# Seven products for eight in 27 groups of the down-projections of a two-block kernel, the sums into the residual shared between VectorE and GpSimd

## The chip, the cores and the metric

The kernel runs on one core of one Trainium2 chip. The metric is the time of one execution on the device in microseconds (us), lower is better; where several executions are given, the median counts. TensorE does the matmuls (PE in the profile, its weight loads PEld), VectorE is DVE, ScalarE is ACT, GpSimd is POOL, and SyncE (SP) issues most of the DMAs.

## The reference, cut to what matters

One sequence of 256 tokens of width 2048 in fp32 goes through two blocks. The first is stick-breaking attention and an MLP with a squared relu, the second is chunked attention beside a pooling branch, and an MLP with a causal convolution of width 3 and a gate:

```python
# first block (D_FF = 8192)
h = h + stick_breaking_mixer(rms_norm(h, norm_mix), sb_w_qkv, sb_w_o)
h = h + jnp.square(jax.nn.relu(rms_norm(h, norm_mlp) @ mlp_w1)) @ mlp_w2
x = rms_norm(h, final_norm)
# second block (D_FF_2 = 5632)
x = x + rms_norm_2(jnp.concatenate([a, p], axis=-1) @ w_o, post_mix_g)
up = causal_dwconv(rms_norm_2(x, pre_ffn_g) @ w_up, conv_w, conv_b)
y = (jax.nn.gelu(up[..., :D_FF_2], approximate=True) * up[..., D_FF_2:]) @ w_down
x = x + rms_norm_2(y, post_ffn_g)
```

The change is in the two down-projections, `mlp_w2` (8192 x 2048) and `w_down` (5632 x 2048), and in what makes their inputs.

## The kernel before

**Tiling.** All weights are streamed from HBM once. The unit is a *piece*: 256 rows of a weight matrix by 512 columns (a *strip* is 512 columns, with 8 pieces for a matrix of 2048 rows). Each weight and each activation is used as two fp32r parts, high and low: ScalarE copies the raw piece, rounded, into `Wh` (L986), and VectorE subtracts to get `Wl` (L1204); together this is the *split* of a piece. A plain piece has 12 matmuls of 128x512: for each row of 128 tokens and each 128 weight rows, high x high, high x low and low x high (`row_products`, through the helper at L1546). The two rows of tokens add up in the two banks of `ps0` or `ps1`; the four banks of `ps2` serve side work.

**Order.** `plan_program` writes the order of all engines by hand: a list of pieces, and steps of each engine that are put `after` a given piece or `later` by some pieces. The plan splits piece i+4 just ahead of the products of piece i. `Wh` and `Wl` have 5 buffers, so a split of piece i waits until piece i-5 has been multiplied, and the raw pieces have 6 buffers, with the load of the next piece into a buffer issued by SyncE once the `Wl` of the last one is there. Every engine works its own steps in order. A step that waits holds up all behind it on its engine.

**Up-projections.** In the first MLP 16 strips of `mlp_w1` are done in chunks of 6, 5 and 5, in the second 11 pairs of strips of `w_up` in chunks of 6 and 5. The output of a strip makes a *trip*: ScalarE stages it in `T0` (L1042 or L1044), two DMAs pass it to DRAM, four DMAs bring it back in another shape (the step `land_rows`, L917), and VectorE transposes it into `T1` (L1256, `turn_strip`). One trip is under way at a time; a trip is landed 3 pieces after its start and turned 4 pieces later. In the first MLP the squared relu is taken on the way and `hid_halves` (L1084, L1325) splits the result into `hid1`. In the second MLP a trip is followed by the convolution, four instructions of ScalarE (L1125) and eight of VectorE (L1416) with one split in between; the first strip of a pair ends in `gelu` (L1129), the second in `gate`, a product of GpSimd (L1529), and `gate_halves` (L1133, L1422) splits its result into `hid2`, two pieces after the gate.

**Down-projections.** After each chunk, four strips of the down-projection use the 12 (or 10) pieces that belong to the chunk, in two pairs of strips (`strip_pair`), and `add_products`, `y_first` or `y_sum` adds the two banks of a strip into the residual `xN` (first MLP, L1283) or into `xn`, which lies in `QK` (second MLP, L1427, L1440). In the second chunk of the second MLP `y_sum` is followed by a product of GpSimd (L1534).

## Time and profile before

| | |
|---|---|
| median of 3 runs | 2095.36 us (2094.35 to 2097.16) |
| the profiled execution | 2095.49 us |
| its span in the profile | 2093.8 us |
| PE busy | 2083.5 us |
| DVE busy | 1224.2 us |
| ACT busy | 1072.2 us |
| POOL busy | 119.7 us |
| read from HBM | 432.75 MB |

The span is the time from the first to the last instruction in the trace; the profiled execution took 1.7 us more than that. A row of a timeline gives start and duration of one instruction, or of several of one form that are merged into a row (x3), and in brackets how long the engine had been idle before it and what ended that wait. Instructions of VectorE that follow each other overlap a little: three splits of 1.23 us stand as 3.49 us. Where the text speaks of the place of piece n after a known time, each plain piece is 12 matmuls.

### The profile page before, as it was taken

Reading aid. Unit: us, or ns where it says so; the run is one execution under the profiler, and the core shown is the slowest. Engines: PE = TensorE matmul, PEld = TensorE weight load, DVE = VectorE, ACT = ScalarE, POOL = GpSimd, SP = SyncE. Lnnn points to the kernel's source line nnn. Section 1 sums busy time; section 2 is a strip of 40 time slices with the busy share of each in tenths; the row PEclk is TensorE's granted clock in tenths of the full one; section 3 lists DMA queues with packets and bytes.
Section 4 is the critical chain, followed back from the end, with each engine's and each line's share of the span. In section 5 each row is a group of like instructions: output and inputs, shape, how many; then the busy total and the mean of one; then the engine's idle time right before and its main releaser. Section 6 shows DMA issues by size and latency. Waiting matters only on the chain.

```text
span 2093.8 us, 23749 instructions
## 1 busy us (share of the span) xinstructions
PE 2083.5 (100%) x9304; PEld 1728.1 (83%) x9304; DVE 1224.2 (58%) x1312; ACT 1072.2 (51%) x1303; POOL 119.7 (6%) x66
## 2 busy tenths in 40 slices
PE   9999999999999999999999999999999999999998
PEld 8888888888888888888888888888888888888887
DVE  6546556655554555455566755566666654566665
ACT  7555654555434543455455554455555533555553
POOL 3000000000000000000002000000112100011120
PEclk9999999999999999999999999999999999999999
DMA  8688666888667885688588777667878766787863
GB/s 297 197 251 236 191 188 216 260 248 235 211 193 206 241 254 194 196 243 238 192 270 232 229 244 232 197 203 211 249 236 250 220 211 193 223 247 242 251 221 121
DMA packets 291903, 469.46 MB, mean 224 GB/s; under 512 B 18512, under 2 KB 82128, under 8 KB 291280
## 3 DMA queue, kind: packets, MB, share of 16 engines
q1 hardware_dynamic: 290928, 463.46, 72.5%
q10 hardware_dynamic: 864, 4.49, 0.6%
q8 instruction: 73, 1.20, 0.2%
q14 instruction: 38, 0.31, 0.0%
HBM read 432.75 MB, written 35.13 MB: 223 GB/s over the span
## 4 chain that ended last, share of the span: by engine, by line
PE 96%; DVE 1%; DMA 1%; ACT 1%; issue 0%; SPq 0%; ACTq 0%; DVEq 0%
PE ps L1546 96%; DMA T<-passed_strip 1%; DVE Wl L1204 0%; DVE zs L1416 0%; ACT Wh L986 0%; DMA E<-passed_rows 0%; DVE T L1256 0%; DMA gains<-in_gains_dram 0%; DVE E L1416 0%; ACT zs L1125 0%; SPq L917 0%; DMA passed_rows<-xN 0%; ACT T L1044 0%; DVE aHL L1307 0%; PE ps L1549 0%
## 5 line engine op out<-in xcount | busy, mean ns | idle before, releaser
L1204 DVE TENSOR_TENSOR Wl<-raw,Wh 128x1024 fp32r<-128x1024 f32 x743 | 908.2, 1242 | 674.2 <-ACT Wh L986 673.6
L1546 PE MATMUL ps<-Wh,aHL 128*128 128x512 f32 x3712 | 1148.8, 390 | 2.4 <-DVE Wl L1204 0.8
L986 ACT ACTIVATE Wh<-raw 128x1024 fp32r<-128x1024 f32 x743 | 768.0, 1054 | 611.1 <-PE ps L1546 608.7
L1546 PEld LDWEIGHTS ps<-Wh,aHL 128*128 128x128 f32 x3712 | 696.8, 188 | 147.9 <-DVE Wl L1204 1.3
L1546 PE MATMUL ps<-Wl,aHL 128*128 128x512 f32 x1856 | 722.1, 389 | 0.0
L1546 PE MATMUL ps<-Wh,hid 128*128 128x512 f32 x1728 | 532.8, 389 | 0.0
L1546 PEld LDWEIGHTS ps<-Wl,aHL 128*128 128x128 f32 x1856 | 348.4, 188 | 71.8
L1546 PEld LDWEIGHTS ps<-Wh,hid 128*128 128x128 f32 x1728 | 324.3, 188 | 67.4
L1546 PE MATMUL ps<-Wl,hid 128*128 128x512 f32 x864 | 336.1, 389 | 0.0
L1546 PEld LDWEIGHTS ps<-Wl,hid 128*128 128x128 f32 x864 | 162.2, 188 | 33.7
L1546 PE MATMUL ps<-Wh,oHL 128*128 128x512 f32 x512 | 159.0, 390 | 0.0
L1546 PEld LDWEIGHTS ps<-Wh,oHL 128*128 128x128 f32 x512 | 96.1, 188 | 20.0
L1529 POOL TENSOR_TENSOR E<-E,zs 128x1024 f32<-128x1024 f32 x11 | 60.9, 5534 | 794.8 <-DVE E L1416 794.8
L1546 PE MATMUL ps<-Wl,oHL 128*128 128x512 f32 x256 | 99.6, 389 | 0.0
L1256 DVE STREAM_TRANSPOSE T<-T 128x1024 f32<-128x1024 f32 x38 | 47.2, 1242 | 17.1 <-DMA T<-passed_strip 17.1
L1546 PEld LDWEIGHTS ps<-Wl,oHL 128*128 128x128 f32 x256 | 48.1, 188 | 9.8
L1044 ACT ACTIVATE T<-ps,rs 128x512 f32<-128x512 f32 x72 | 46.0, 676 | 15.6 <-PE ps L1546 7.9
L1520 POOL TENSOR_TENSOR QK<-E 128x1020 f32<-128x1020 f32 x2 | 3.8, 1886 | 821.6 <-DVE E L1256 821.6
L1125 ACT ACTIVATE E<-T,conv 128x256 f32<-128x256 f32 x44 | 22.9, 590 | 44.5 <-DVE T L1256 44.5
L1133 ACT ACTIVATE hid<-E 128x1024 fp32r<-128x1024 f32 x11 | 11.7, 1061 | 65.6 <-POOL E L1529 65.6
L1125 ACT ACTIVATE zs<-T,conv 128x256 f32<-128x256 f32 x44 | 22.9, 590 | 31.9 <-DVE T L1256 31.9
L1084 ACT ACTIVATE hid<-T 128x1024 fp32r<-128x1024 f32 x16 | 17.0, 1062 | 39.2 <-DVE T L1256 39.2
(167 smaller groups left out, 687.4 us busy)
## 6 DMA issues: line engine op xcount, KB each, us to landing
raw<-in_mlp_w_dram SPq DMA_DIRECT2D x256, 512.0 KB, 4.5
raw<-in_w_up_dram SPq DMA_DIRECT2D x176, 512.0 KB, 4.6
raw<-in_sb_w_qkv_dram SPq DMA_DIRECT2D x93, 512.0 KB, 5.2
raw<-in_w_down_dram SPq DMA_DIRECT2D x88, 512.0 KB, 4.7
raw<-in_w_in_dram SPq DMA_DIRECT2D x64, 512.0 KB, 4.8
passed_strip<-T SPq DMA_DIRECT2D x104, 256.0 KB, 4.5
T<-passed_strip SPq DMA_DIRECT2D x208, 128.0 KB, 5.2
raw<-in_sb_w_o_dram SPq DMA_DIRECT2D x32, 512.0 KB, 5.4
```

Of the source, the lines that this page charges most:

```text
L986: e.activation(Wh[:, i % NW, :], rawv[:, i % NRAW, :], ACT.Copy).then_inc(st["hi"][0], 1)
L1044: e.activation(strip_rows[:, t, :], ps[st["set"]][:, t, :], ACT.Copy, scale=cols[st["col"]][:, t:t + 1]).then_inc(st["staged"][t][0], 1)
L1084: e.activation(hid1[:, st["t0"]:st["t0"] + 4, 0:TOK], T1[:, :, :], ACT.Copy).then_inc(st["hi"][0], 1)
L1125: e.activation(C[:, m, :], T1[:, m, :], ACT.Identity, scale=conv[:, 2, n0 + m:n0 + m + 1], bias=conv[:, 3, n0 + m:n0 + m + 1]).then_inc(st ...
L1133: e.activation(hid2[:, st["t0"]:st["t0"] + 4, 0:TOK], E4, ACT.Copy).then_inc(st["hi"][0], 1)
L1204: e.tensor_tensor(Wl[:, i % NW, :], rawv[:, i % NRAW, :], Wh[:, i % NW, :].bitcast(F32), ALU.subtract).then_inc(st["lo"][0], 1)
L1256: e.transpose(dst, strip_blocks).then_inc(st["done"][0], 1)
L1520: e.tensor_tensor(dst[:, a:4, sh:TOK], src[:, a:4, sh:TOK], src[:, a:4, 0:TOK - sh], ALU.add).then_inc(added[0], 1)
L1529: e.tensor_tensor(E4, E4, Z4, ALU.mult).then_inc(st["done"][0], 1)
L1546: return e.matmul(o, l, r, start=start, stop=stop, skip_group_check=True)
```

## The change

A *group* takes one pair of pieces, the same 256 weight rows of two neighbouring strips (a, b), and computes their eight half products (two rows of tokens, two halves of the 256 weight rows, two strips) as seven products of sums, in the manner of Strassen and Winograd. It is four entries in the list of pieces: `s0`, `s1`, `s2` with 6 matmuls each and `s3` with 3, together 21 where two plain pieces have 24. There are 27 groups: three in each pair of strips of every chunk of both down-projections, but for the last pair of `mlp_w2`. Groups are spaced by 3 or 2 plain pieces.

Around a group the change adds:

- `weight_sums`: four additions of 128x512 on VectorE, from the two raw pieces into the new tile `wsum` (the second writes into the raw piece), ahead of the split of `s0`; `s1` to `s3` are split from these sums (`s2` 1024 wide, `s3` 512 wide).
- `mix_tokens` and `mix_low`: the sums of the activations, four instructions of VectorE, one of ScalarE and one more of VectorE, once for groups 0 and 1 of a chunk (`n=2`) and once for group 2 (`n=1`); they stand behind `hid_halves` and `gate_halves` of the first two results of a chunk. `gate_halves` itself moves back by a piece in all rounds.
- `fold`: the four banks of `ps2`, in which the groups of a pair of strips add up, are brought into the residual: one copy by ScalarE, and eight additions. In the 7 folds that add to a residual, VectorE makes five and GpSimd three (`fold_rest`); in the two of the first chunk of `w_down`, which begin `xn`, VectorE makes all. `add_products`, `y_first` and `y_sum` wait for the fold, and the next `weight_sums` or `mix_tokens` wait for it too.
- the row factor of the first MLP is applied in the relu, and no longer as its square in `add_products`.

The core of the diff:

```diff
@@ strip_pair, seven @@
+    def strip_pair(w, s4, ks, tail, mov, tiles, evacs, koff=0, sevens=(), fold=None):
+        plain = [kp for kp in ks if kp not in sevens]
...
+        lead, gap = (4, 3) if tail else (2, 3 if len(plain) > 7 else 2)
+        rest = a[lead:n] + b[:n] if tail else a[lead:n - 1] + b[:2] + a[n - 1:] + b[2:]
+        p.pieces[first:] = a[:lead]
+        for m, kp in enumerate(sevens):
+            seven(w, s4, kp, mov, tiles, (a[0]["strip"], b[0]["strip"]), koff, m, m == 0, fold if m == len(sevens) - 1 else None)
+            p.pieces += rest[gap * m:gap * m + gap] if m < len(sevens) - 1 else rest[gap * m:]
+        p.pieces += a[n:] + b[n:] if tail else []
...
+        for i, kind in enumerate(("s0", "s1", "s2", "s3")):
+            src = (w, "rows", kp * 256, (s4 + i) * STRIP) if i < 2 else None
@@ evac_relu and gated @@
+                if t0 < 8:
+                    free["T1"] = [lo, mix_tokens("hid1", "T1", t0 // 2, 2 if t0 == 0 else 1, [turned])]
...
+                    if t0 < 8:
+                        free["E"] = [lo, mix_tokens("hid2", "E", t0 // 2, 2 if t0 == 0 else 1, [g])]
                     hid_tiles[t0:t0 + 4] = [lo] * 4
-                later(2, halves)
+                later(3, halves)
@@ the pairs of mlp_w2 and w_down @@
+                           sevens=() if c == 2 and s4 else tuple(range(2 * at, 2 * at + 3)), fold=fold_into("xN", s4))
...
+                           sevens=tuple(range(2 * at, 2 * at + 3)), fold=fold_into("xn", s4, fresh=c == 0))
@@ vector_program @@
+                elif k == "weight_sums":
...
+                    e.tensor_tensor(wsum[:, 0, :], a[:, 0, :], b[:, 0, :], ALU.add).then_inc(made[1][0], 1)
+                    e.tensor_tensor(b[:, 0, :], b[:, 0, :], b[:, 1, :], ALU.add).then_inc(made[3][0], 1)
+                    e.wait_ge(*made[1])
+                    e.tensor_tensor(wsum[:, 1, :], wsum[:, 0, :], b[:, 1, :], ALU.add).then_inc(made[2][0], 1)
+                    e.wait_ge(*made[2])
+                    e.tensor_tensor(wsum[:, 2, :], wsum[:, 1, :], a[:, 1, :], ALU.add).then_inc(made[4][0], 1)
+                elif k == "mix_tokens":
...
+                    e.tensor_tensor(d[:, :, 1, :], even[:, :, 0:128], even[:, :, 128:256], ALU.subtract).then_inc(st["d"][0][0], 1)
+                    e.tensor_tensor(d[:, :, 0, :], even[:, :, 128:256], odd[:, :, 128:256], ALU.subtract).then_inc(st["d"][1][0], 1)
...
+                    e.wait_ge(*st["d"][2])
+                    e.tensor_tensor(d[:, :, 3, :], d[:, :, 2, :], odd[:, :, 0:128], ALU.add).then_inc(st["d"][3][0], 1)
+                elif k == "mix_low":
...
+                    e.tensor_tensor(lo, d, hi.bitcast(F32), ALU.subtract).then_inc(st["lo"][0], 1)
+                elif k in ("fold", "fold_rest"):
...
+                        e.tensor_tensor(wsum[:, 0, :], P[:, 0, :], wsum[:, 0, :], ALU.add).then_inc(m[0][0], 1)
...
+                            e.tensor_tensor(x[:, 0, a], x[:, 0, a], P[:, 0, :], ALU.add).then_inc(m[1][0], 1)
+                            e.wait_ge(*m[0])
+                            e.tensor_tensor(wsum[:, 1, :], P[:, 2, :], wsum[:, 0, :], ALU.add).then_inc(m[2][0], 1)
+                            e.tensor_tensor(wsum[:, 2, :], P[:, 1, :], wsum[:, 0, :], ALU.subtract).then_inc(m[3][0], 1)
...
+                        e.tensor_tensor(wsum[:, 0, :], P[:, 1, :], wsum[:, 1, :], ALU.subtract).then_inc(m[4][0], 1)
@@ scalar_program @@
+                elif k == "fold":
...
+                    e.activation(wsum[:, 0, :], ps[2][:, 3, :], ACT.Copy).then_inc(st["copied"][0], 1)
+                elif k == "mix_tokens":
+                    d, hi, lo = mixed_rows(st)
+                    e.wait_ge(*st["d"][3])
+                    e.activation(hi, d, ACT.Copy).then_inc(st["hi"][0], 1)
@@ pool_program @@
+                elif k == "fold_rest" and not st["fresh"]:
...
+                    e.wait_ge(*m[2])
+                    e.tensor_tensor(x[:, 1, a], x[:, 1, a], wsum[:, 1, :], ALU.add).then_inc(added[0][0], 1)
+                    e.wait_ge(*m[3])
+                    e.tensor_tensor(x[:, 0, b], x[:, 0, b], wsum[:, 2, :], ALU.add).then_inc(added[1][0], 1)
+                    e.wait_ge(*m[4])
+                    e.tensor_tensor(x[:, 1, b], x[:, 1, b], wsum[:, 0, :], ALU.add).then_inc(added[2][0], 1)
@@ tensor_program @@
+                terms = {"s0": (("a11", side[:, 0, :], q["opens"], True), ("a12", a[:, 0, :], False, False)),
+                         "s1": (("d1", side[:, 2, :], q["opens"], True), ("d3", b[:, 0, :], q["opens"], False)),
+                         "s2": (("d0", side[:, 1, :], q["opens"], True), ("d2", side[:, 3, :], q["opens"], True)),
+                         "s3": (("a22", a[:, 1, :], False, False),)}[q["kind"]]
+                for t, (name, P, starts, ends) in enumerate(terms):
+                    c = slice(t * 512, (t + 1) * 512)
+                    x, h, l = halves_of[name]
+                    mm(P, x[:, h:h + 128], wh[:, c], starts, False)
+                    mm(P, x[:, h:h + 128], wl[:, c], False, False)
+                    m = mm(P, x[:, l:l + 128], wh[:, c], False, ends and q["closes"])
```

**How the steps stand on VectorE, first place.** These are VectorE's instructions in the first round of `w_up`, before. The convolutions into `E` and then into `zs` belong to the second strip of the first pair and the first strip of the second; `hid<-E` is `gate_halves`, and `Wl<-raw,Wh` are splits.

```order
L1416 SCALAR_TENSOR_TENSOR E<-T,conv,E 128x254 x2
L1204 TENSOR_TENSOR Wl<-raw,Wh 128x1024 x3
L1422 TENSOR_TENSOR hid<-E,hid 128x4x256
L1204 TENSOR_TENSOR Wl<-raw,Wh 128x1024 x3
L1256 STREAM_TRANSPOSE T<-T 128x1024
L1204 TENSOR_TENSOR Wl<-raw,Wh 128x1024
L1416 SCALAR_TENSOR_TENSOR zs<-T,conv,zs 128x255 x2
```

The same place in the changed kernel:

```order
L1578 SCALAR_TENSOR_TENSOR E<-T,conv,E 128x254 x2
L1323 TENSOR_TENSOR Wl<-raw,Wh 128x1024 x4
L1584 TENSOR_TENSOR hid<-E,hid 128x4x256
L1341 TENSOR_TENSOR wsum<-E 128x2x128
L1342 TENSOR_TENSOR wsum<-E 128x2x128
L1344 SCALAR_TENSOR_TENSOR wsum<-wsum,E 128x2x128
L1347 TENSOR_TENSOR wsum<-wsum,E 128x2x128
L1323 TENSOR_TENSOR Wl<-raw,Wh 128x1024
L1351 TENSOR_TENSOR hidMix<-wsum,hidMix 128x8x128
L1323 TENSOR_TENSOR Wl<-raw,Wh 128x1024
L1422 STREAM_TRANSPOSE T<-T 128x1024
L1323 TENSOR_TENSOR Wl<-raw,Wh 128x1024
```

One split has moved ahead of `gate_halves`, and the five instructions of the mix stand between it and the transpose. On ScalarE, whose order at that place is the second piece, the high part of the mix stands ahead of the next two splits:

```order
L1251 ACTIVATE hid<-E 128x4x256
L1103 ACTIVATE hidMix<-wsum 128x8x128
L1099 ACTIVATE Wh<-raw 128x1024 x2
L1243 ACTIVATE zs<-T,conv 128x256 x4
L1099 ACTIVATE Wh<-raw 128x1024
```

Before, three splits stood there between the first row and the four of the convolution, and no mix.

**Second place.** VectorE where the first `w_down` begins, before: the last trip of the chunk (transpose, split, convolution), its gate's halves, and then splits up to `y_first`.

```order
L1256 STREAM_TRANSPOSE T<-T 128x1024
L1204 TENSOR_TENSOR Wl<-raw,Wh 128x1024
L1416 SCALAR_TENSOR_TENSOR E<-T,conv,E 128x255 x2
L1416 SCALAR_TENSOR_TENSOR E<-T,conv,E 128x254 x2
L1416 SCALAR_TENSOR_TENSOR E<-T,conv,E 128x255 x2
L1416 SCALAR_TENSOR_TENSOR E<-T,conv,E 128x254 x2
L1204 TENSOR_TENSOR Wl<-raw,Wh 128x1024 x3
L1422 TENSOR_TENSOR hid<-E,hid 128x4x256
L1204 TENSOR_TENSOR Wl<-raw,Wh 128x1024 x11
```

The same place in the changed kernel, from the four sums of the second group on:

```order
L1422 STREAM_TRANSPOSE T<-T 128x1024
L1329 TENSOR_TENSOR wsum<-raw 128x512
L1330 TENSOR_TENSOR raw<-raw 128x512
L1332 TENSOR_TENSOR wsum<-wsum,raw 128x512
L1334 TENSOR_TENSOR wsum<-wsum,raw 128x512
L1323 TENSOR_TENSOR Wl<-raw,Wh 128x1024
L1578 SCALAR_TENSOR_TENSOR E<-T,conv,E 128x255 x2
L1578 SCALAR_TENSOR_TENSOR E<-T,conv,E 128x254 x2
L1578 SCALAR_TENSOR_TENSOR E<-T,conv,E 128x255 x2
L1578 SCALAR_TENSOR_TENSOR E<-T,conv,E 128x254 x2
L1323 TENSOR_TENSOR Wl<-raw,Wh 128x1024
L1323 TENSOR_TENSOR Wl<-wsum,Wh 128x1024
```

The last transpose now falls just ahead of the second group's sums, and the whole convolution stands between the splits of that group's `s0` and `s1`. `hid<-E` follows behind the splits of `s1`, `s2`, `s3` and one plain piece.

## Rows read from the trace of the kernel before

**Rows 1.** The page, part 1: busy time of each engine, share, instructions.

```profile
PE 2083.5 (100%) x9304; PEld 1728.1 (83%) x9304; DVE 1224.2 (58%) x1312; ACT 1072.2 (51%) x1303; POOL 119.7 (6%) x66
```

**Rows 2.** Waits of PE: who was waited for, us in total, times, longest.

```profile
PE ps L1546 <- DVE Wl L1204: 0.8, 1, 0.8
```

**Rows 3.** The chain that ended last, in order of time: start, us, what.

```profile
1464.97 620.47 PE ps L1546 x2736
```

**Rows 4.** Groups of VectorE and ScalarE by form: busy us, mean ns, idle before.

```profile
L1204 DVE TENSOR_TENSOR Wl<-raw,Wh 128x1024 fp32r<-128x1024 f32 x743 | 908.2, 1242 | 674.2 <-ACT Wh L986 673.6
...
L1286 DVE TENSOR_TENSOR xN<-xN,ps 128x512 f32<-128x512 f32 x8 | 5.1, 681 | 0.0
```

**Rows 5.** Timeline of VectorE in the first round of w_up.

```profile
1443.35 3.49 DVE L1204 TENSOR_TENSOR Wl<-raw,Wh 128x1024 fp32r<-128x1024 f32 x3
1450.22 1.23 DVE L1422 TENSOR_TENSOR hid<-E,hid 128x1024 fp32r<-128x1024 f32 x1 [3.38 <-ACT hid L1133]
...
1455.05 1.25 DVE L1256 STREAM_TRANSPOSE T<-T 128x1024 f32<-128x1024 f32 x1 [0.20 <-DMA T<-passed_strip]
...
1460.54 3.24 DVE L1416 SCALAR_TENSOR_TENSOR zs<-T,conv,zs 128x255 f32<-128x255 f32 x8
1463.69 1.22 DVE L1204 TENSOR_TENSOR Wl<-raw,Wh 128x1024 fp32r<-128x1024 f32 x1
```

**Rows 6.** Timeline of ScalarE at the same place.

```profile
1449.12 1.06 ACT L1133 ACTIVATE hid<-E 128x1024 fp32r<-128x1024 f32 x1 [7.26 <-POOL E L1529]
```

**Rows 7.** Timeline of PE at the end of that stretch.

```profile
1464.97 0.50 PE L1546 MATMUL ps<-Wh,aHL 128*128 128x512 f32 x1 [0.84 <-DVE Wl L1204]
```

**Rows 8.** Timeline of VectorE: the split behind the convolution, in three later rounds.

```profile
1505.70 1.22 DVE L1204 TENSOR_TENSOR Wl<-raw,Wh 128x1024 fp32r<-128x1024 f32 x1
...
1852.31 1.22 DVE L1204 TENSOR_TENSOR Wl<-raw,Wh 128x1024 fp32r<-128x1024 f32 x1
...
1895.22 1.23 DVE L1204 TENSOR_TENSOR Wl<-raw,Wh 128x1024 fp32r<-128x1024 f32 x1
```

**Rows 9.** Timeline of GpSimd: first and last gate of the first chunk.

```profile
1444.00 5.09 POOL L1529 TENSOR_TENSOR E<-E,zs 128x1024 f32<-128x1024 f32 x1 [288.90 <-DVE E L1416]
...
1658.87 5.58 POOL L1529 TENSOR_TENSOR E<-E,zs 128x1024 f32<-128x1024 f32 x1 [39.02 <-DVE E L1416]
```

**Rows 10.** Timeline of GpSimd: an addition of 128x1020.

```profile
1122.86 1.89 POOL L1520 TENSOR_TENSOR QK<-E 128x1020 f32<-128x1020 f32 x1 [805.04 <-DVE E L1256]
```

**Rows 11.** Timeline of VectorE: a split that begins inside that GpSimd instruction.

```profile
1123.12 2.71 DVE L1204 TENSOR_TENSOR Wl<-raw,Wh 128x1024 fp32r<-128x1024 f32 x1 [0.34 <-ACT Wh L986]
```

**Rows 12.** Timeline of VectorE from the last trip of the first chunk of w_up.

```profile
1650.06 1.25 DVE L1256 STREAM_TRANSPOSE T<-T 128x1024 f32<-128x1024 f32 x1 [2.86 <-DMA T<-passed_strip]
1654.41 1.22 DVE L1204 TENSOR_TENSOR Wl<-raw,Wh 128x1024 fp32r<-128x1024 f32 x1 [3.10 <-ACT Wh L986]
1655.55 3.24 DVE L1416 SCALAR_TENSOR_TENSOR E<-T,conv,E 128x255 f32<-128x255 f32 x8
1658.70 3.49 DVE L1204 TENSOR_TENSOR Wl<-raw,Wh 128x1024 fp32r<-128x1024 f32 x3
```

**Rows 13.** Timeline of SyncE: landing DMAs of the last trip of each chunk.

```profile
1640.26 1.97 SPq L917 DMA_DIRECT2D T<-passed_strip  x4
...
1987.35 2.57 SPq L917 DMA_DIRECT2D T<-passed_strip  x4
```

**Rows 14.** Timeline of VectorE: the transpose behind the second of them.

```profile
1996.42 1.25 DVE L1256 STREAM_TRANSPOSE T<-T 128x1024 f32<-128x1024 f32 x1 [1.06 <-DMA T<-passed_strip]
```

**Rows 15.** The page, part 6: DMAs of one line, KB each, median us to landing.

```profile
T<-passed_strip SPq DMA_DIRECT2D x208, 128.0 KB, 5.2
```

**Rows 16.** GpSimd: products and sums of 128x512, by form.

```profile
L1534 POOL TENSOR_TENSOR QK<-QK,g_row 128x512 f32<-128x512 f32 x6 | 7.7, 1298 | 43.4 <-ACT T L1139 43.4
L1494 POOL TENSOR_TENSOR E<-E 128x512 f32<-128x512 f32 x2 | 3.7, 1828 | 24.2 <-ACT E L990 24.2
```

**Rows 17.** Timeline of VectorE: a transpose in the first MLP.

```profile
467.81 1.24 DVE L1256 STREAM_TRANSPOSE T<-T 128x1024 f32<-128x1024 f32 x1
```

227 lines of the change are left out of this document (173 added, 54 removed).

## The prediction

> **What bounds the kernel now.** The page's busy times come first: PE is busy for 2083.5 us of a span of 2093.8, DVE for 1224.2 [rows 1]. Next the waits of PE: in the middle of the program there is one of note, 0.8 us on the low half of a weight piece [rows 2]. So the kernel is bound by the number of matmuls. Their price is in the chain of waits: 2736 of them in a row take 620.47 us [rows 3], 0.2268 us each, and a plain piece of 12 takes 2.721 us with no loss between pieces. That row also gives a clock for the text: piece n after 1464.97 starts at 1464.97 + 2.721 n. The last thing to read is who is nearly late. VectorE splits a piece in 1.15 us when splits follow each other (three in 3.49 [rows 5]; 1.24 alone [rows 4]), under half of what PE takes for it, but its queue is in order, and in each round of `w_up` it waits for a DMA, for ScalarE and for GpSimd in turn. The reader should look there for the slack, not at the share of 58%.
>
> **What is removed.** A group has 21 matmuls for 24: 27 x 3 = 81 matmuls x 0.2268 = **18.4 us less** on PE. PE has no other work to put there, so the whole of it is on the path as long as each split is there in time. Loads from HBM are unchanged. The weights of a group reach VectorE and ScalarE as two raw pieces as before.
>
> **What is added where it is hidden.** Four sums of 128x512 cost 0.68 each alone, as the nearest additions do [rows 4], some 2.5 together. `s2` and `s3` add a split of 1.15 and one of half the size, 0.6. That is 4.2 us more on VectorE for each group. Between groups: with three plain pieces PE takes 4.76 + 8.16 = 12.9 us and VectorE 10.0, with two 10.2 and 8.9. Both fit, so a row of groups by itself takes no time. In the order of the buffers the tightest split (the first plain one behind `s3`, which waits for the piece five before it) is ready some 2.4 us early. The first groups of the first MLP meet a transpose and its halves, VectorE's queue being some 7.3 us long from the transpose to the split of `s0`. The transpose needs no wait at 467.81, 18.6 us behind its strip's end [rows 17]; here it can start at 15.8, so the split ends at 23.1, and PE wants it at 23.8: nothing lost, 0 to 1 us for all three chunks. The sums of the activations in the first MLP are hidden too, since there the splits run a full four pieces ahead. The relu of the first MLP now takes the row factor as a scale, on ScalarE, which has room there: no cost on the path.
>
> **The fold.** ScalarE's copy and VectorE's five additions read PSUM. GpSimd's three are 1.30 each at the best and 1.83 on average in the worst row [rows 16]. Here the two engines shut each other out: a split that begins 0.26 us into a GpSimd addition takes 2.71 instead of 1.23, and ends 1.1 after that addition [rows 10, 11]. And GpSimd gets nothing done while splits of VectorE follow each other: the gate at 1658.87 takes 5.58 us, of which three splits fill the first 3.3 (to 1662.19), and it ends 2.26 after them [rows 9, 12]. So three additions on GpSimd (3.9) take more of what the engines share than on VectorE (1.8 to 2.0). The Trainium skill (*GPSIMD Engine Reference*, section 4.1, Engine selection) speaks against this move: element-wise work with two inputs belongs on VectorE, GpSimd being about twice as slow. By that factor and the 0.68 of rows 4 an estimate is 4.1 us for the three against the 3.9 of rows 16, and the sum below would stay. Who waits: `add_products`, with VectorE's whole queue behind it. Before the last two groups' pairs that matter (second chunk of each MLP, where only two plain pieces lie between the fold and `add_products`) I reach: additions done 9.8 us after the fold's start, the sums at 13.6, `s0` split at 14.8 against 16.3, `s2` at 18.3 against 19.1. Slack 0.8: **0 us**, bounds 0 and 4 (two places x 2).
>
> **The first mix in `w_up` (n=2).** Here nothing is hidden, since PE already waits 0.84 [rows 7] for the split behind the convolution [rows 5]. `gate_halves` stands one split later. ScalarE's part of it begins when GpSimd is done, at 1449.12 [rows 6]; the gate takes from 1444.00 to there [rows 9], 2.26 behind the third split. Now a fourth split follows without a gap, its high part being long ready, so the gate ends 1.15 later. Then, on VectorE: low half of the gate to 1452.5; the four sums at 0.4 to 0.5 (the eight of the convolution take 3.24 [rows 5]) to 1454.3; ScalarE's high part of the mix 1.06 and the high part of the next split 1.0, both exposed, to 1456.3; split to 1457.6, low part of the mix to 1458.7, split to 1459.9. The transpose starts 4.8 us later than at 1455.05, and all behind it too. PE loses **4.8** (3.6 if the gate is not held).
>
> The second mix (n=1) has half the width or less: 3.5 late by the same steps. The split behind its convolution ends at 1506.92 and PE wants it at 1508.51 [rows 8]: slack 1.6, loss **1.9** (0.8 to 1.9). In the second chunk the split ends at 1853.53, with PE at 1464.97 + 144 x 2.721 = 1856.85: slack 3.3 [rows 8], loss **1.5** (0 to 1.7). The fourth would have 3.9 [rows 8], but after a round with no slack the trips are late, and the first chunk shows that a round wins back 1.6: loss between 0 and 1.9, I take **1.0**. Together 9.2.
>
> **The last trip against the second group of `w_down`.** Before, the first `w_down` starts at 1464.97 + 60 x 2.721 = 1628.25. Its last trip is transposed at +21.8, and the split behind the convolution ends 9.8 after that, at +31.6, with PE there at +32.7 [rows 12]. Slack 1.0. In the change PE comes to the same place in VectorE's queue (`s1` of the second group) after 7 plain pieces, 21 matmuls and the 6 of `s0`, at +25.2, or 7.5 us sooner. The trip lands earlier as well, since fewer pieces stand ahead of it on SyncE: by the steps above the split of the first group's `s1` ends at +12.0, and the landing DMAs go then (before: at +12.0 in the first chunk, +10.8 in the second [rows 13]; there I find 10.7). From first issue to the transpose it is 9.8 and 9.1 [rows 12 to 14], at least 2.0 + 5.2 = 7.2 [rows 13, 15]. With two loads just ahead instead of three I take 8: the transpose L is at +20.1 and +18.7. The four sums hide behind ScalarE's half of the convolution, so `s1` is there at L + 9.9: 4.8 and 3.4 late. Then the gate: four splits follow each other (4.1 us), GpSimd needs 2.25 behind them, ScalarE 1.1 for the halves and 1.0 for the next split, VectorE's low halves the rest, which makes L + 18.6 for a piece that PE would want at +31.3. The second wait comes on top: in all L - 12.7, or **7.4** and **6.0**, 13.4 us (bounds: L from 17.2 in both, 9.0; L of 21.9 and 19.7, 16.2).
>
> **The sum.** Against the profiled execution, 2095.5 (span 2093.8, and 1.7 around it, 0.1 above the median of 2095.36): 2095.5 - 18.4 + 9.2 + 13.4 = 2099.7, and with 0.3 for the first MLP **2100**. The gain is real and PE hands all of it back waiting for VectorE.
>
> **The rivals.**
> 1. *The lead holds.* If trips land at L = 17.2, the gates are not held back by a fourth split and the three later mixes stay in their slack, the losses are 3.6 + 0.8 + 0.4 + 9.0 = 13.8, which gives 2091; with no wait at all it is 2077. For it: PE's waits before were a single 0.84, and I count every wait from durations of one trace. Against it: the 7.5 us by which PE arrives sooner are sure. Chance 0.22, 2077 to 2091.
> 2. *GpSimd's three additions become the bound.* In the two places with two plain pieces ahead of `add_products`, a slower addition moves `s2` past PE, from a lateness of 0.8 us on. At 1.83 each [rows 16] the three end 1.6 later and a place loses 0.8; at 2.7, as long as the split that was shut out [rows 11], it loses 3.4. Two such places and landings at 9.8 give 2104 to 2110. Chance 0.13. It ends slower.
> 3. *Entries of 3 and 6 matmuls do not run at the pitch of 12.* Rows 3 show no loss at a boundary, which speaks against it; at 0.1 us for each of 54 more boundaries 2105. Chance 0.05.
> 4. The forecast, 2093 to 2106, chance 0.60.
>
> **How the numbers follow.** A measurement of this kernel can tell about 0.2%, 4.2 us: from 2091.2 to 2099.6 is no change. The forecast lies just above that bound; of its 0.60 I give 0.28 to the same and 0.32 to slower. Rival 1 is faster, rivals 2 and 3 slower: faster 0.22, same 0.28, slower 0.50. The range takes in most of rival 1's upper end and rival 2: 2088 to 2108.
>
> **What would show it.** PE's matmuls fall by 81, its busy time by some 18 if waits are not counted as busy. PE's waits should name the low half of the weights four times in `w_up` (4.8 first) and twice in each `w_down`, behind the convolution (3 to 5) and behind `gate_halves` (2 to 3). The first gate should take 6.2 instead of 5.1 us, and transposes behind a mix come 3.5 to 5 later against PE. The forecast is wrong if the second group's `s1` is there before PE, if ScalarE's mix does not hold its next split, or if `add_products` waits for GpSimd until PE runs dry.

## The result and the profile after

The changed kernel takes **2123.9 us** (median of 4 runs, 2122.3 to 2126.9) where the kernel before, timed beside it, takes 2096.3: a ratio of 1.0133, with a 95% interval of 1.0115 to 1.0150. It is 28 us slower. The forecast was 2100, in a range of 2088 to 2108: the sign was the likelier one, the size was not.

The page of the changed kernel, part 1, against [rows 1]: 81 matmuls fewer, VectorE 169 us busier, GpSimd 52 us busier. The span is 2120.5.

```profile
PE 2082.5 (98%) x9223; PEld 1717.3 (81%) x9223; DVE 1393.3 (66%) x1568; ACT 1129.4 (53%) x1376; POOL 171.6 (8%) x87
```

PE's busy time hardly fell (2083.5 to 2082.5), though 81 matmuls at 0.2268 should take 18.4 off it. That is the first sign of something besides the waits shown. PE's waits, against the single one of [rows 2]:

```profile
PE ps L1722 <- DVE Wl L1323: 26.2, 19, 4.7
PE ps L1722 <- DVE QK L1606: 2.9, 2, 2.4
```

The row of 620 us without a break [rows 3] is gone. In the chain of waits of the changed kernel other engines stand between shorter rows of matmuls (start, us, what):

```profile
1645.39 9.27 DMA T<-passed_strip
1660.25 3.17 DVE E L1578 x8
1663.48 6.17 POOL E L1705
1673.19 159.43 PE ps L1722 x702
```

**Where it went.** The trace gives the number of matmuls up to any time. The time lost in a stretch is how much later the last of its matmuls comes, with 0.2268 us credited for each one that the change saved before it (readings from windows 2.5 us apart, good to some 0.3 us, and to 0.8 where a wait falls between two stretches; what the kernel before itself lost counts as zero, so its own wait of 0.84 can show as a gain). The same for the experiments that are told below:

| us lost in | change | fold on VectorE | mixes alone | groups in first MLP only | w_down: second pair only | w_down: first pair only | third chunk plain | causes removed |
|---|---|---|---|---|---|---|---|---|
| first MLP, chunks 1 and 2 | 1.1 | 0.0 | 0.0 | 1.6 | 2.0 | 1.6 | 1.1 | 1.1 |
| third chunk, pair 1 | 1.8 | 0.7 | 0.2 | 0.0 | 0.3 | 0.5 | 0.0 | 0.0 |
| third chunk, pair 2 | 4.1 | 3.7 | -0.2 | -0.2 | 4.3 | 3.9 | -0.2 | -0.2 |
| w_up, chunk 1 | 7.1 | 6.2 | 8.0 | -1.1 | 6.8 | 6.6 | 6.2 | 7.1 |
| w_down, chunk 1, pair 1 | 10.7 | 9.1 | 0.2 | 1.6 | 0.1 | 10.7 | 9.1 | 1.6 |
| w_up, chunk 2 | 1.7 | 3.1 | 4.4 | 0.1 | 2.8 | 3.1 | 5.6 | 1.9 |
| w_down, chunk 2, pair 1 | 11.6 | 12.0 | 1.6 | 0.2 | 1.8 | 15.5 | 13.2 | 0.0 |
| w_down, chunk 2, pair 2 | 7.6 | 5.7 | 0.1 | 0.3 | 2.6 | -0.2 | 8.1 | 1.9 |

What is left of each column (attention, the second pair of the first chunk of w_down) is a gain of 0.5 to 1.0 in all. In the change everything comes to 44.8; less 18.4 it is 26.4 of the 26.7 us between the two spans.

The 1.8 in the first pair of the third chunk is a wait of PE of 1.26 at 989.46, 18 us before that pair's fold. The last trip of the chunk landed late there: VectorE waited 1.63 for the DMA before its transpose at 982.04, with the sums and the split of a group behind it. Five other kernels run the same program up to there (experiments 4, 6, 7, 9 and 13), and in their traces PE has no wait over 0.2 at that place. So it belongs to this one execution, and not to the fold.

**The first mix** in w_up, against [rows 5] to [rows 7]. Timelines of GpSimd, VectorE and PE in the changed kernel (start, us, engine, line, what, and in brackets the idle time before it and what ended that):

```profile
1439.31 6.56 POOL L1705 TENSOR_TENSOR E<-E,zs 128x1024 f32<-128x1024 f32 x1 [287.36 <-DVE E L1578]
1447.00 1.23 DVE L1584 TENSOR_TENSOR hid<-E,hid 128x1024 fp32r<-128x1024 f32 x1 [3.38 <-ACT hid L1251]
1451.77 1.23 DVE L1323 TENSOR_TENSOR Wl<-raw,Wh 128x1024 fp32r<-128x1024 f32 x1 [2.08 <-ACT Wh L1099]
1455.18 1.24 DVE L1422 STREAM_TRANSPOSE T<-T 128x1024 f32<-128x1024 f32 x1
1453.05 0.50 PE L1722 MATMUL ps<-Wh,aHL 128*128 128x512 f32 x1 [0.85 <-DVE Wl L1323]
1460.80 0.80 PE L1722 MATMUL ps<-Wh,aHL 128*128 128x512 f32 x1 [2.00 <-DVE Wl L1323]
```

The gate begins 4.7 us sooner than before and takes 6.56 instead of 5.09; the transpose stands at 1455.18 and not at 1455.05, so it has lost 4.8 us to the gate, as forecast. PE waits 2.85 in all there, and the stretch loses 4.1: the clock, told below, takes another 1.7.

**The start of the first w_down**, against [rows 12] and [rows 13]. PE comes to 1631.4 there. Timelines of SyncE (the landing DMAs of the last trip), VectorE, then PE:

```profile
1643.90 1.95 SPq L1024 DMA_DIRECT2D T<-passed_strip  x4
1654.69 1.25 DVE L1422 STREAM_TRANSPOSE T<-T 128x1024 f32<-128x1024 f32 x1 [6.10 <-DMA T<-passed_strip]
1659.03 1.23 DVE L1323 TENSOR_TENSOR Wl<-raw,Wh 128x1024 fp32r<-128x1024 f32 x1 [0.59 <-ACT Wh L1099]
1663.32 1.22 DVE L1323 TENSOR_TENSOR Wl<-raw,Wh 128x1024 fp32r<-128x1024 f32 x1
1660.40 0.76 PE L1722 MATMUL ps<-Wh,hid 128*128 128x512 f32 x1 [4.74 <-DVE Wl L1323]
1664.60 0.80 PE L1722 MATMUL ps<-Wh,hidMix 128*128 128x512 f32 x1 [1.30 <-DVE Wl L1323]
```

The two splits are those of the second group's `s0`, with the four sums ahead of it, and of its `s1`, with the convolution ahead of it. The first matmul behind each wait takes 0.76 and 0.80 where 0.50 is usual. The windows around it tell why (from:to, length, busy time and count of PE, PEld, DVE, ACT and POOL, granted clock of TensorE, DMA share, GB/s):

```profile
1650.00:1658.00 8.00, 5.66 (x25) 4.34 (x24) 3.28 (x5) 2.03 (x5) 0.00 (x0) 1.00 0.72 209
1658.50:1669.00 10.50, 7.30 (x16) 5.30 (x17) 8.39 (x13) 3.86 (x5) 5.51 (x1) 0.51 0.34 107
1669.00:1680.00 11.00, 10.90 (x48) 8.67 (x47) 9.19 (x10) 7.42 (x8) 0.65 (x1) 1.00 0.48 157
```

The granted clock falls from 1.00 to 0.50, that is from 2.4 to 1.2 GHz, in the middle of the wait and stays there until 1669: 16 matmuls in 7.3 us where full speed makes twice as many. That is 3.6 us lost on top of the waits. In windows of half a microsecond the same shows in three other places: 1460.8 to 1464.2, 2017.2 to 2024.0 and 2102.5 to 2105.9. The kernel before has it only at its very end. Half of the matmul time in them is 1.7, 2.5 and 1.7: together with the 3.6 some **9.5 us**, a fifth of the 44.8 lost, and one half of why PE's busy time did not fall. No term of the forecast had it.

**The fold of the third chunk**, where the next pair has no group. Timelines of GpSimd, VectorE, PE:

```profile
1011.03 1.29 POOL L1697 TENSOR_TENSOR xN<-xN,wsum 128x512 f32<-128x512 f32 x1 [167.81 <-DVE wsum L1366]
1012.29 2.27 POOL L1699 TENSOR_TENSOR xN<-xN,wsum 128x512 f32<-128x512 f32 x1
1014.52 2.27 POOL L1701 TENSOR_TENSOR xN<-xN,wsum 128x512 f32<-128x512 f32 x1
1013.93 1.71 DVE L1323 TENSOR_TENSOR Wl<-raw,Wh 128x1024 fp32r<-128x1024 f32 x1
1016.99 1.29 DVE L1448 TENSOR_TENSOR xN<-xN,ps 128x512 f32<-128x512 f32 x2 [1.35 <-PE ps L1722]
1020.10 1.23 DVE L1323 TENSOR_TENSOR Wl<-raw,Wh 128x1024 fp32r<-128x1024 f32 x1 [1.82 <-ACT Wh L1099]
1024.34 1.23 DVE L1323 TENSOR_TENSOR Wl<-raw,Wh 128x1024 fp32r<-128x1024 f32 x1 [1.81 <-ACT Wh L1099]
1028.58 1.23 DVE L1323 TENSOR_TENSOR Wl<-raw,Wh 128x1024 fp32r<-128x1024 f32 x1 [1.82 <-ACT Wh L1099]
1029.86 0.50 PE L1722 MATMUL ps<-Wh,hid 128*128 128x512 f32 x1 [0.36 <-DVE Wl L1323]
```

`add_products` (L1448) is put down as waiting for PE, but the strip's last matmul ended at about 1012.7; what ended at 1016.79 is GpSimd's third addition. From there on VectorE splits a piece only every 4.24 us, since each split stands behind an addition and, on ScalarE, behind the squares of its result; PE takes one every 2.72 and catches up at 1029.86. The kernel before runs the same chain, but its `add_products` begins at 1019.97, as soon as the strip is done, and so the chain has four to five more microseconds in hand. GpSimd's first addition takes 1.29, its second and third 2.27, in this fold as in all seven.

**The last pair of w_down**: the same chain with `y_sum`, in two places. At the front of the pair it is `y_sum` of the pair before, behind that pair's fold, with this pair's first group in it. The first wait of PE is for `y_sum` itself: a group writes the sums of both strips, and so needs early the banks that `y_sum` still reads. Timelines of VectorE, ScalarE, PE:

```profile
2050.38 1.29 DVE L1606 TENSOR_TENSOR QK<-QK,ps 128x512 f32<-128x512 f32 x2 [1.28 <-POOL QK L1701]
2058.60 1.28 DVE L1606 TENSOR_TENSOR QK<-QK,ps 128x512 f32<-128x512 f32 x2
2059.31 0.63 ACT L1257 ACTIVATE T<-QK 128x512 f32<-128x512 f32 x1 [4.24 <-DVE QK L1606]
2061.84 2.52 DVE L1323 TENSOR_TENSOR Wl<-wsum,Wh 128x1024 fp32r<-128x1024 f32 x2 [1.96 <-ACT Wh L1099]
2059.93 0.50 PE L1722 MATMUL ps<-Wh,hid 128*128 128x512 f32 x1 [2.44 <-DVE QK L1606]
2063.81 0.50 PE L1722 MATMUL ps<-Wh,hidMix 128*128 128x512 f32 x1 [0.85 <-DVE Wl L1323]
```

Near its end it is the pair's own fold, whose last addition on GpSimd ends at 2095.92, and the `y_sum` behind it. Timelines of VectorE and PE:

```profile
2096.92 1.27 DVE L1606 TENSOR_TENSOR QK<-QK,ps 128x512 f32<-128x512 f32 x2
2100.16 1.88 DVE L1323 TENSOR_TENSOR Wl<-raw,Wh 128x1024 fp32r<-128x1024 f32 x1 [1.96 <-ACT Wh L1099]
2102.09 0.50 PE L1722 MATMUL ps<-Wh,hid 128*128 128x512 f32 x1 [1.95 <-DVE Wl L1323]
```

This wait, with the 1.7 of half clock behind it, is 3.8 of the 7.6 us, one half.

### The profile page after: what moved, and what is told of

Its sections match the earlier page's. It is cut to its first block, busy times and chain, and to the rows that moved or that the text cites. A ratio compares the mean times of both kernels' runs of the same rounds, so it can differ in the third digit from the quotient of the medians.

```text
span 2120.5 us, 24084 instructions
## 1 busy us (share of the span) xinstructions
PE 2082.5 (98%) x9223; PEld 1717.3 (81%) x9223; DVE 1393.3 (66%) x1568; ACT 1129.4 (53%) x1376; POOL 171.6 (8%) x87
## 4 chain that ended last, share of the span: by engine, by line
PE 75%; DVE 10%; DMA 5%; ACT 4%; issue 2%; POOL 2%; SPq 1%; ACTq 0%; DVEq 0%; POOLq 0%
PE ps L1722 75%; DVE Wl L1323 4%; DMA T<-passed_strip 4%; ACT Wh L1099 2%; POOL E L1705 2%; DVE E L1578 1%; DVE zs L1578 1%; DVE T L1422 1%; SPq L1024 1%; ACT zs L1243 1%; ACT E L1243 0%; ACT hid L1251 0%; DMA passed_rows<-xN 0%; SPq L1045 0%; DVE wsum L1332 0%
## 5 line engine op out<-in xcount | busy, mean ns | idle before, releaser
L1722 PE MATMUL ps<-Wh,hid 128*128 128x512 f32 x1458 | 461.5, 392 | 19.4 <-DVE Wl L1323 16.1
L1722 PEld LDWEIGHTS ps<-Wh,hid 128*128 128x128 f32 x1458 | 275.1, 189 | 83.8 <-issue 12.9
L1722 PE MATMUL ps<-Wl,hid 128*128 128x512 f32 x729 | 285.1, 391 | 0.0
L1722 PEld LDWEIGHTS ps<-Wl,hid 128*128 128x128 f32 x729 | 137.7, 189 | 28.1
L1705 POOL TENSOR_TENSOR E<-E,zs 128x1024 f32<-128x1024 f32 x11 | 71.5, 6499 | 802.3 <-DVE E L1578 802.3
L1722 PE MATMUL ps<-Wh,hidMix 128*128 128x512 f32 x216 | 74.2, 405 | 4.1 <-DVE Wl L1323 4.1
L1099 ACT ACTIVATE Wh<-wsum 128x1024 fp32r<-128x1024 f32 (+1 forms) x54 | 44.1, 838 | 26.5 <-PE ps L1722 26.0
L1722 PEld LDWEIGHTS ps<-Wh,hidMix 128*128 128x128 f32 x216 | 42.3, 196 | 15.0 <-DVE Wl L1323 5.9
L1323 DVE TENSOR_TENSOR Wl<-wsum,Wh 128x1024 fp32r<-128x1024 f32 (+1 forms) x54 | 50.3, 966 | 6.3 <-ACT Wh L1099 6.3
```

The source lines that it names most:

```text
L1099: e.activation(Wh[:, i % NW, c], src, ACT.Copy).then_inc(st["hi"][0], 1)
L1323: e.tensor_tensor(Wl[:, i % NW, c], src, Wh[:, i % NW, c].bitcast(F32), ALU.subtract).then_inc(st["lo"][0], 1)
L1705: e.tensor_tensor(E4, E4, Z4, ALU.mult).then_inc(st["done"][0], 1)
L1722: return e.matmul(o, l, r, start=start, stop=stop, skip_group_check=True)
```

## The experiments

All are built from the changed kernel unless the text says otherwise, and each was timed beside the kernel before.

**1. All additions of a fold on VectorE.** This undoes what gives the change its name, and no more.

```diff
@@ vector_program, fold_rest @@
                         e.tensor_tensor(wsum[:, 0, :], P[:, 1, :], wsum[:, 1, :], ALU.subtract).then_inc(m[4][0], 1)
+                        e.tensor_tensor(x[:, 1, a], x[:, 1, a], wsum[:, 1, :], ALU.add).then_inc(added[0][0], 1)
+                        e.tensor_tensor(x[:, 0, b], x[:, 0, b], wsum[:, 2, :], ALU.add).then_inc(added[1][0], 1)
+                        e.wait_ge(*m[4])
+                        e.tensor_tensor(x[:, 1, b], x[:, 1, b], wsum[:, 0, :], ALU.add).then_inc(added[2][0], 1)
```

> The changed kernel with all eight additions of a fold on VectorE. Theory 1 (GpSimd's additions and VectorE shut each other out, and that is a third of what was lost): the fold's additions end earlier in the second chunk of w_down, its second pair of strips loses 2 to 4 us and not 7.6, the last pair of the first MLP's third chunk 2 and not 4.1, and the time is 2114 to 2119. Theory 2 (what is late is VectorE's whole queue, and three more additions of 0.7 us there cost what GpSimd's cost): 2122 to 2127. The losses in the rounds of w_up (4.1 and 3.0) and at the start of the first w_down (10.7) stay in both, since no fold with GpSimd stands there.

Measured: 2118.05, ratio 1.0109 (1.0095 to 1.0122) against 1.0133: **5 to 6 us back**, theory 1 in the total. By the table at most 3.4 of it lie where additions of GpSimd are waited for (1.1 in the first two chunks, 0.4 in the third chunk's second pair, 1.9 in the last); the rest moved too: 2.5 less in w_up and w_down of the first chunk, where GpSimd adds nothing, 1.1 less in the wait at 989.46, and 1.8 more in the second chunk up to the end of its first pair. The fold of the third chunk in this kernel, timeline of VectorE, where the additions take 0.69 each and `add_products` (now L1453) follows without a wait, 2.9 us sooner than in the change:

```profile
1011.72 0.69 DVE L1377 TENSOR_TENSOR xN<-xN,wsum 128x512 f32<-128x512 f32 x1
1012.32 0.69 DVE L1379 TENSOR_TENSOR xN<-xN,wsum 128x512 f32<-128x512 f32 x1
1012.92 1.22 DVE L1323 TENSOR_TENSOR Wl<-raw,Wh 128x1024 fp32r<-128x1024 f32 x1
1014.05 1.28 DVE L1453 TENSOR_TENSOR xN<-xN,ps 128x512 f32<-128x512 f32 x2
```

But the two pairs still lose 3.7 and 5.7, not 2 and 2 to 4. PE too is 2.3 us sooner here, so little of that lead is kept, and the chain of splits at 4.24 us is late whoever adds. GpSimd is at most a fifth of the loss, not a third.

**2. The mixes alone.** No group at all; the sums of the activations are made and not used, and `gate_halves` stays a piece later. (`sevens=()` in both down-projections.)

> The changed kernel with every group replaced by its two plain pieces, the sums of the activations kept (made and not used), gate_halves still a piece later. Theory 1 (the sums of the activations are late by themselves): w_up loses 4.1 + 3.0 + 1.7 = 8.8 us as it does with groups, and where w_down begins there is no wait over 1 us, which gives 2096.3 + 8.8 - 0.8 = 2104. Theory 2 (they only cost together with groups, since it is the groups of the first MLP that use up the lead): 2096 to 2098, with no wait over 1.5 us in w_up.

Measured: 2108.8, ratio 1.0066 (1.0053 to 1.0080): **13.6 us** over the kernel before, more than either theory gave. No group is needed for the loss in w_up. It is 8.0 in the first chunk, and in the second 4.4 where the change itself lost 1.7, with 1.6 more where w_down begins. Two of PE's waits in this kernel:

```profile
1463.77 0.50 PE L1725 MATMUL ps<-Wh,aHL 128*128 128x512 f32 x1 [1.98 <-DVE Wl L1323]
1468.07 0.50 PE L1725 MATMUL ps<-Wh,aHL 128*128 128x512 f32 x1 [1.25 <-DVE Wl L1323]
```

**3. Groups in the first two chunks of the first MLP only**: 12 of 27, and no mixes in w_up.

```diff
-                           sevens=() if c == 2 and s4 else tuple(range(2 * at, 2 * at + 3)), fold=fold_into("xN", s4))
+                           sevens=() if c == 2 else tuple(range(2 * at, 2 * at + 3)), fold=fold_into("xN", s4))
...
-                           sevens=tuple(range(2 * at, 2 * at + 3)), fold=fold_into("xn", s4, fresh=c == 0))
+                           sevens=(), fold=fold_into("xn", s4, fresh=c == 0))
...
-                    if t0 < 8:
+                    if t0 < 0:
                         free["E"] = [lo, mix_tokens("hid2", "E", t0 // 2, 2 if t0 == 0 else 1, [g])]
...
-                later(3, halves)
+                later(2, halves)
```

> Groups in the first and second chunk of the first MLP's down-projection alone (12 of the 27), no group and no sums of activations elsewhere, gate_halves where it was before. Theory 1 (a group that meets slack gives its 0.68 us back whole, and these 12 do): 36 matmuls less, 2096.3 - 8.2 = 2088, with no new wait of PE. Theory 2 (part of what was lost later was brought on by these groups, by loads and trips that come out of step): 2091 to 2096, with waits in the third chunk at 989 and 1030 to 1052.

Measured: **2087.5** (2087.1 to 2089.2), ratio 0.9963 (0.9949 to 0.9976). Theory 1. It beats both kernels, the one before by 7.7 us where its 36 matmuls are worth 8.2. VectorE's weights hold PE up for

```profile
PE ps L1725 <- DVE Wl L1323: 1.2, 1, 1.2
```

and the clock shows no fall.

**4. Groups in w_down's second pairs only**: the six groups of the first pairs plain (`sevens=() if s4 == 0 else ...`).

> The changed kernel with the six groups of the first pair of strips plain in both chunks of w_down, the rest as it was. Theory 1 (the 10.7 and 11.6 us lost where a w_down begins come from the groups that meet the last trip and its gate there): 6 x 0.68 = 4.1 us more matmuls, 20 to 22 us less waiting, 2104 to 2108, and no granted clock at its lower level where w_down begins. Theory 2 (they come from the trips and gate_halves being late already behind w_up's sums of activations): 2122 to 2128, the wait of 4.7 us still there. The 7.6 us of the second chunk's second pair stay in both.

Measured: 2102.8, ratio 1.0034 (1.0021 to 1.0048). Theory 1, and a little more: 4.1 us of matmuls come back in and the time still falls by 21, so **25 us** of loss go with the six groups. The starts of w_down lose 0.1 and 1.8, the granted clock stays at 1.00 there, and the last pair loses 2.6, not 7.6, though its own groups stay. That part of the expectation missed: the 7.6 did not stay. What is left is the wait behind the pair's own fold, again 1.95 long (at 2082.65), this time with no fall of the clock.

**5. `gate_halves` a piece later, in the kernel before, and nothing else** (`later(2, halves)` to `later(3, halves)`).

> The kernel before with one edit: gate_halves a piece later, in all rounds. The sums of the activations with this edit, without groups, cost 13.6 us. Theory 1 (the sums themselves cost that; the later gate_halves only holds the first gate by one more split, 1.15 us, where PE already waited 0.84): 2096 to 2098. Theory 2 (gate_halves moved past a split is late in every round and takes a good part of the 13.6): 2100 to 2104, with waits of PE in most rounds of w_up.

Measured: 2096.2 against 2095.8, ratio 1.0002 (0.9993 to 1.0011). Theory 1: no cost. The 13.6 of experiment 2 are the mixes' own.

**6. `gate_halves` back in its place, in the changed kernel** (`later(3, halves)` to `later(2, halves)`).

> The changed kernel with gate_halves where it was before (two pieces after the gate, not three), the groups and the sums of the activations as they are. Theory 1 (the later place costs the gate 1.15 us a time): the gates take 5.5 us again and the time is 2119 to 2123. Theory 2 (the sums of the activations, which move with gate_halves, then stand in front of a split that is nearer to PE): 2124 to 2130, w_up loses more than 4.1 and 3.0.

Measured: 2129.2, ratio 1.0160 (1.0147 to 1.0174). Theory 2: 5 us slower than the change. The later place, which the forecast charged with 1.2 us a gate, is worth 5 us where mixes follow.

**7. The first group of the last pair behind three plain pieces, not two.**

```diff
-        lead, gap = (4, 3) if tail else (2, 3 if len(plain) > 7 else 2)
+        lead, gap = (4, 3) if tail else (3 if w == "w_down_2" and koff else 2, 3 if len(plain) > 7 else 2)
```

> The changed kernel with the first group of the second chunk's second pair of strips in w_down behind three plain pieces, not two. A group opens the sums of its second strip, so PE needs the PSUM tile that y_sum of the pair before still reads; PE waited 2.4 us there for y_sum, and 0.9 for the split behind it. Theory 1 (that early need is the cause of half of the 7.6 us lost in this pair): the wait on y_sum is under 0.5, and the time is 2119 to 2122. Theory 2 (the split of s2 behind y_sum's squares on ScalarE is late by itself, and PE waits for that in place of y_sum): 2123 to 2126.

Measured: 2126.9, ratio 1.0153 (1.0140 to 1.0167). Theory 2, and 0.9 above its range; the profiled execution is a long one, 2132.7. The wait on `y_sum` shrinks, and another takes its place behind it:

```profile
2067.56 0.50 PE L1722 MATMUL ps<-Wh,hid 128*128 128x512 f32 x1 [0.23 <-DVE QK L1606]
2071.40 0.50 PE L1722 MATMUL ps<-Wh,hidMix 128*128 128x512 f32 x1 [2.19 <-DVE Wl L1323]
```

**8. Holds of VectorE, in the kernel before.** A row of dependent additions of 352 elements (0.56 us each) in six places of the down-projections, so that one split is late.

```diff
+                elif k == "hold":
+                    held = spare[:, 0:352].rearrange("p (a b) -> p a b", a=4)
+                    e.wait_ge(*st["conv"])
+                    for d in st["held"]:
+                        e.tensor_tensor(held, conv[:, :, :], conv[:, :, :], ALU.add).then_inc(d[0], 1)
+                        e.wait_ge(*d)
```

> The kernel before with six holds of VectorE in the down-projections of the first and second chunk, each a row of dependent additions of 352 elements, 22, 24, 25, 26, 28 and 34 of them, so that the split behind it is late and PE waits a length that differs from hold to hold, from near 0 to some 6 us. Nothing else is changed. Theory 1 (a long wait of PE makes its granted clock fall from 2.4 to 1.2 GHz, and the matmuls behind it pay for that besides the wait): behind waits of 4 us or more the clock is at its lower level for some us and the time lost there is 3 to 5 us more than the wait; behind short ones it is not. Theory 2 (the low clock in the changed kernel came from several waits close together, not from a single one): no low clock behind any hold, and each costs its wait alone.

PE's six waits:

```profile
557.95 0.50 PE L1554 MATMUL ps<-Wh,hid 128*128 128x512 f32 x1 [2.31 <-DVE Wl L1206]
614.48 0.79 PE L1554 MATMUL ps<-Wh,hid 128*128 128x512 f32 x1 [4.55 <-DVE Wl L1206]
807.39 0.50 PE L1554 MATMUL ps<-Wh,hid 128*128 128x512 f32 x1 [3.43 <-DVE Wl L1206]
863.94 0.80 PE L1554 MATMUL ps<-Wh,hid 128*128 128x512 f32 x1 [5.66 <-DVE Wl L1206]
1705.13 0.80 PE L1554 MATMUL ps<-Wh,hid 128*128 128x512 f32 x1 [9.24 <-DVE Wl L1206]
1776.54 0.79 PE L1554 MATMUL ps<-Wh,hid 128*128 128x512 f32 x1 [9.02 <-DVE Wl L1206]
```

Behind the wait of 2.31 the clock stays at 1.00, and the stretch loses 2.5. Behind or within the five others it falls to 0.50, and the stretches lose 6.4, 5.3, 7.3, 11.8 and 11.7: the wait and **1.6 to 2.7 us more**. Theory 1, with an extra smaller than the 3 to 5 expected. In total 2143.9, ratio 1.0227 (1.0213 to 1.0241). Two windows, before the end of the longest wait's low stretch and behind it:

```profile
1705.00:1709.50 4.50, 4.37 (x10) 3.47 (x11) 4.50 (x5) 0.00 (x0) 0.00 (x0) 0.50 0.56 188
1710.00:1715.00 5.00, 5.00 (x23) 4.10 (x22) 1.91 (x2) 2.12 (x2) 0.00 (x0) 1.00 0.96 351
```

**9. Groups in w_down's first pairs only**, the mirror of experiment 4.

> The changed kernel with the six groups of the second pair of strips plain in both chunks of w_down; the mirror of the run with groups in the second pair only. Groups there cost matmuls of 6 x 0.68 = 4.1 us when plain. Theory 1 (the 7.6 us lost in the second chunk's second pair come from the fold of the pair before, which makes y_sum and its squares late, so plain pieces lose there too, as in the third chunk of the first MLP): it still loses 3 to 5 us, and the time is 2123 to 2126. Theory 2 (they come from this pair's own groups, whose splits stand behind the squares): it loses under 1 us, and the time is 2119 to 2121.

Measured: 2121.3, ratio 1.0122 (1.0107 to 1.0138). Theory 2: the last pair loses nothing when it is plain, though the fold stands before it. (The start of this chunk loses 15.5 here and not 11.6, so the total is no better than it is.) With experiment 4 that makes the front of the pair a loss of two together: it takes the fold ahead and the groups. The end of the pair needs the pair's own groups and fold, and those alone.

**10. The first MLP's third chunk plain.**

> The changed kernel without the three groups of the first MLP's third chunk, which it has in the first pair of strips alone. PE lost 1.8 us in that pair and 4.1 in the next, where no group stands. Theory 1 (the fold of these three groups holds add_products, and with it the chain of sums, squares and splits that fills the next pair): both losses go, for 2.0 us of matmuls, and the time is 2119 to 2121. Theory 2 (VectorE is behind there from the second chunk on): the losses stay and the time is 2125 to 2127.

Measured: 2121.9, ratio 1.0131 (1.0117 to 1.0146), between the two. In the trace both losses of the chunk are gone, as theory 1 has it. `add_products` begins at 1012.83 there, at the end of its strip, and not 4 us behind it: the fold had held it. (The 1.8 of the first pair was not the fold's, as said above.) But the second chunk of w_up and the w_down behind it lose 5.5 us more than in the change, those of the first chunk 2.5 less.

**11. Mixes of later strips, alone.** As experiment 2, but the third and fourth result of each chunk are mixed, where [rows 8] made me see more slack.

```diff
-                    if t0 < 8:
-                        free["E"] = [lo, mix_tokens("hid2", "E", t0 // 2, 2 if t0 == 0 else 1, [g])]
+                    if 8 <= t0 < 16:
+                        free["E"] = [lo, mix_tokens("hid2", "E", (t0 - 8) // 2, 2 if t0 == 8 else 1, [g])]
```

> As mixes_alone (no groups at all, sums of the activations made and not used), but in w_up the sums are those of the third and fourth strip of hid2 in each chunk, not of the first and second; as many instructions, later. Theory 1 (a mix costs what it takes beyond the slack of its round, and a round wins back 1.6 us): the slack there is some 3 us more than in the first rounds, so the 13.6 us fall to 4 to 7, that is 2100 to 2103. Theory 2 (a mix costs the same wherever it stands, through the buffer that holds up the next trip or the gate): 2107 to 2110.

Measured: 2108.5, ratio 1.0059 (1.0046 to 1.0073), the same as with the first strips. Theory 2: later rounds have no slack to give either. (These are rounds still later than those of [rows 8].) From 1520 to 1628 on the clock of before this kernel loses 8.1 us.

**12. The version of experiment 3 with its folds on VectorE.**

> The version with groups in the first two chunks of the first MLP only (2087.5), and with all eight additions of its three or four folds on VectorE. Theory 1 (where a fold has slack it does not matter who adds): within 1.5 us of the same version with GpSimd, 2086 to 2089. Theory 2 (GpSimd's additions cost here too, 1 us in the second chunk, whose second pair has two plain pieces behind its fold): 2085 to 2086.5.

Measured: 2088.4 (2086.2 to 2089.7), ratio 0.9964 (0.9951 to 0.9976), theory 1. Where PE does not wait behind a fold, it makes no difference who adds.

**13. One group in each first pair of w_down.**

> The changed kernel with one group, the first, in the first pair of strips of each w_down, and the second and third of that pair plain; three in the second pair as in the change. Against the run with groups in the second pair only (2102.8) it has 2 x 0.68 = 1.4 us less to multiply and two folds more; the one of the second chunk stands before y_sum, and there the second pair should lose 7.6 us again and not 2.6. Theory 1 (it is the second group that meets the last trip and its gate; the first is innocent): the stretches where w_down begins lose under 2 us each (10.7 and 11.6 in the change), no granted clock at the lower level there, and the time is 2105 to 2108. Theory 2 (a first group is enough, since PE comes sooner to the splits behind the trip): they lose 4 us or more each, 2112 to 2118.

Measured: 2122.4, ratio 1.0117 (1.0100 to 1.0134): theory 2 by its stretches, which lose 10.0 and 10.7, and 4 us above its range in time. Part of that is w_up's second chunk, which loses 7.1 here and 2.8 in experiment 4. The last pair loses 3.9, and not 7.6 again as expected: only the wait of 1.95 behind its own fold and the half clock. A fold that comes earlier in the pair ahead costs nothing at the front. PE's waits where the first w_down begins:

```profile
1644.35 0.47 PE L1725 MATMUL ps<-Wh,hid 128*128 128x512 f32 x1 [2.17 <-DVE Wl L1323]
1661.02 0.47 PE L1725 MATMUL ps<-Wh,hid 128*128 128x512 f32 x1 [1.88 <-DVE Wl L1323]
1667.01 0.50 PE L1725 MATMUL ps<-Wh,hid 128*128 128x512 f32 x1 [1.42 <-DVE Wl L1323]
```

The test is not as clean as meant: a lone group closes its sums, so its fold falls where the last trip is transposed and stands between the splits there. What it shows is that the loss doesn't need the second group; any group and fold between the last trip and its gate brings it.

**14. The found causes removed**: third chunk plain, w_down's first pairs plain, folds on VectorE; 18 groups and all mixes stay.

> The changed kernel with what the runs have named taken out, and the sums of the activations of w_up left in: no groups in the first MLP's third chunk and in w_down's first pairs, all additions of a fold on VectorE; 18 groups stay. Theory 1 (the costs are separate and add up; what then remains is the 13.4 us of the sums of the activations in w_up): 2095.8 - 18 x 0.68 + 13.4 + some 2 for the second chunk's last pair = 2099, 2097 to 2101. Theory 2 (they are not separate: part of each was covered by another, for instance the sums of the activations cost less where PE had lost time before): 2102 to 2106.

Measured: 2097.0, ratio 1.0006 (0.9997 to 1.0016). Theory 1, at the low end of its range. What is left after the 12.2 us that 18 groups save is a loss of 13.4 us, near the 13.6 of experiment 2, but not in the same places: w_up loses 9.0 here and 12.4 there, and the last pair 1.9, with a wait of 1.44 behind its own fold. So the costs nearly add up, though not place by place, and what is left, most of it in w_up with its mixes, eats what 18 groups save.

## Why the prediction failed, step by step

- **Removed work: right.** 81 matmuls at 0.2268 are 18.4 us; 36 of them alone gave 7.7 of their 8.2 us back in experiment 3. Entries of 3 and 6 matmuls run at the pitch of 12 (rival 3 falls), and the first MLP's 12 groups are hidden, as worked out, to about 1 us; the forecast had 0.3 for its three chunks, and a late landing in the third made it 2.9 in this execution.
- **The mixes in w_up: the total right, in part by luck.** Forecast 9.2, measured 8.8. Of the four, the first lost 4.1 (4.8), the second 3.0 (1.9), the two of the second chunk 1.7 (2.5). Of the 4.1 another 1.7 is half clock, which the forecast did not have, so the waits there were shorter than worked out. The transpose came 4.8 later against the gate, as said, and the first gate took 6.56 (6.2). In the second chunk PE loses nothing behind the first mix (1.5), neither in the change nor in experiment 2, so the slack of 3.3 read from [rows 8] was there and more than enough. All of the chunk's loss comes behind the second mix: 1.7 in the change and 4.4 in experiment 2, some 3 of them in that round and the rest later, where the forecast took 1.0 against a slack of 3.9. That slack was wrong, and experiment 11 found none in later rounds. The later `gate_halves` costs nothing (experiment 5) and saves 5 us beside the mixes (experiment 6).
- **The last trip against w_down's groups: the mechanism right, its term L mis-sized.** The forecast was L - 12.7, with L, the transpose's time after w_down's start, at 20.1 and 18.7. It came at 1654.69, 23.3 after 1631.4, and at 2010.77, 22.8 after 1988.0. L - 12.7 with these is 10.6 and 10.1; measured 10.7 and 11.6, the second with 1.4 us of waiting already at the first group. So the failed sentence is "the trip lands earlier as well": the first of its landing DMAs went at +12.5 and +13.9, where the forecast had +12.0 and +10.7, and from there to the transpose it was 10.8 and 8.9 us, not 8. In the first chunk it was the DMAs that took longer, in the second they went later. My bound for L, 21.9 and 19.7, was too low too. How the 10.7 is made up differs as well: 6.0 us of waits and 3.6 of half clock, the first wait was already for the group's `s0`, and the second forecast wait, behind `gate_halves`, did not come. That PE at 1.2 GHz got there later fits experiment 1, with as much waiting before it (5.98), 3.4 us at half clock in place of 10.2 and then a wait of 0.54 at 1668.23; no run held the clock fixed. And by experiment 13 it is not the second group alone.
- **The fold at 0 us: the step that failed most.** It cost 4.1 in the third chunk and, together with the groups behind it, 7.6 in the last pair, 11.7 together, beyond my bound of 4. That the additions end 9.8 us after the fold began was right (9.0 from ScalarE's copy at 1007.81 to 1016.79). I took the bound from the two places in the second chunks, and followed VectorE's queue only to the next group's splits. In the third chunk no group follows, so I didn't look; but there `add_products` is the head of a chain over ScalarE's squares that makes a split every 4.24 us, and its lead over PE had been four to five us larger. In the last pair two things were not followed: that the first group needs the banks which `y_sum` reads (a wait of 2.44), and the chain behind the pair's own fold (a wait of 1.95). The 7.6 also hold 1.7 of half clock. Of rival 2 the price was right (2.27 for an addition, between 1.83 and 2.7), its places half right: `y_sum` did wait 1.28 for GpSimd in w_down, but nothing came in the first MLP's second chunk.
- **That GpSimd and VectorE shut each other out** was read rightly from [rows 10, 11]. The Trainium skill (*SBUF — State Buffer*, section "SBUF: two separate sides") has it that the pair of ports which the two share is taken whole for one instruction, and the other engine waits; the trace agrees, with 1.29 us for the addition that begins ahead of a split and 2.27 for those that meet one, and 1.71 for the split between the last two. Yet undoing that part brings only 5 to 6 of the 28 us.
- **The clock: not in the forecast at all**, some 9.5 us in four places. It is not a cause beside the waits but their surcharge, and where it stands it hides part of a wait that would have followed.
- **What the profile should have shown.** Waits on the low half of the weights four times in w_up: five (0.85, 2.00, 0.72, 1.26, 1.28). Twice in each w_down: two in the first, five where the second begins. PE's busy time some 18 us less: 1.0. `add_products` waiting for GpSimd until PE runs dry was named as what would prove the forecast wrong, and it did.
- The sum by these: -18.4 + 8.8 + 22.3 + 11.7, and 2.9 for trips against groups in the first MLP less 0.9 elsewhere, is 26.4 where the spans differ by 26.7. Of the 22 us between the forecast and the profiled execution (2122.3), the fold is 11.7 and the last trip 8.9.

What stays open: why the mixes of the second chunk cost 1.7 in the change, 4.4 alone, 5.6 in experiment 10 and 7.1 in experiment 13; the trips there land at other times in each kernel, and no run here held them fixed.

## What to carry to other kernels

A saving on the engine that bounds is worth its whole size only where the feeding engine's queue has slack to the end of its chain; count the groups that sit there (12 of 27 here, -7.7 us) and leave out the rest, which saved 10 us here and cost 47. When a step is made later, follow its queue and the next engine's queue until the lead is whole again, not until the next event of the change. And charge a wait of the matmul engine of some 3.5 us or more, and some of those from 2 us on, with 2 to 4 us more for its clock.

## What was not expected of the hardware

- The granted clock fell to its lower level behind the holds' waits of 3.43 to 9.24 us, and not behind the one of 2.31; yet in the changed kernel it also fell behind one of 2.00 us (with one of 0.85 some 6 us ahead of it) and behind a lone one of 1.95, and with the folds on VectorE not behind one of 2.01. The lone wait of 1.95 in the last pair, in the same place of the program, brought it in the change and in experiments 10 and 13, and not in experiment 4. These runs don't tell what decides there. The low stretch lasted some 3.4 us behind the holds' waits of up to 5.66, 6.8 with the pair of 2.86 and 1.91, and 10.2 with the holds' waits of 9 and with the pair of 4.74 and 1.30.
- The cost of a wait can begin behind its end: the wait of 3.43 ended at 807.39 and the clock fell at 808.8.
- A wait costs 0.17 more than its row shows, by the starts of the matmuls on both sides of it: the 2.31 are 2.48, the 0.84 of [rows 7] are 1.00. Over the 24 waits of the change above 0.2 us that is some 4 us. Another 4 are starts that lie some 0.1 us further apart than 0.2268 with no wait shown. With the 9.5 of the clock that is why PE's busy time did not fall.
